# Beginning of a two-block kernel rebuilt: small modulation products, operands kept in PSUM, w_in chunks started earlier and in another order; attention part of the second block reordered

## The reference

```
# first block
mx = silu(c) @ ada_w + ada_b           # six modulation vectors of 1024: shift, scale, gate, ...
mc = silu(c_ctx) @ ada_w + ada_b       # only shift and scale are needed
hx = rmsnorm(x) * (1 + scale_x) + shift_x ;  hc = the same with ctx and mc
u = h @ w_in                           # q, forget gates (both directions), values, fourier part, gates
o = hgrn_bidir(...)                    # scan over x, started with the end states of a scan over ctx
y = (sigmoid(ga) * (fourier(u) @ w_a) + sigmoid(gb) * (readout(o) @ w_b)) @ w_out ; x = x + gate * y
x = x + gate2 * conv_ffn(modulate(rmsnorm(x), shift2, scale2)) ; x = rmsnorm(x)
# second block
p = rmsnorm(x) @ w_in_2                # q, k, v, three parts of a short convolution, u for pooling
mix = [band attention(q, k, v), short convolution, multiscale pooling(u)]
x = x + mix @ w_out_2 ; x = x + relu(rmsnorm(x) @ w_mlp1)**2 @ w_mlp2
```

## Time and profile before

| | us |
|---|---|
| median of 3 executions | 785.23 |
| fastest, slowest | 782.67, 795.02 |
| the profiled execution, its own time | 794.74 |
| its span in the trace | 792.9 |
| mean granted TensorE clock of the span | 0.976 |

### The profile page before, as it was taken

How to read it: one execution, slowest core, us unless ns; L and a number is a source line. 1 busy time by engine, 2 the same in 40 slices (tenths; PEclk the granted TensorE clock), 3 DMA queues, 4 the chain that set the end, 5 groups by cost and what they waited for, 6 DMA issues and landing times.

```text
span 792.9 us, 14202 instructions
## 1 busy us (share of the span) xinstructions
PE 748.9 (94%) x5892; PEld 715.1 (90%) x5892; DVE 548.5 (69%) x900; ACT 354.1 (45%) x417; POOL 434.0 (55%) x317
## 2 busy tenths in 40 slices
PE   8779999999989989999996998999699999999998
PEld 3468899999989989999996998999699999999998
DVE  5989994687563548987898878144965755565563
ACT  5445333454542555555534455434455433343331
POOL 0257642678679769899895987674738400000000
PEclk9889999999999989999998999999999999999999
DMA  9944345423676446446526554442315466545611
GB/s 376 420 163 173 143 179 213 161 84 131 215 263 211 150 169 246 160 167 259 216 104 266 229 198 165 152 160 107 112 59 203 150 224 212 169 176 187 213 54 54
DMA packets 20661, 144.63 MB, mean 182 GB/s; under 512 B 2291, under 2 KB 2547, under 8 KB 3445
## 3 DMA queue, kind: packets, MB, share of 16 engines
q1 hardware_dynamic: 20448, 143.64, 49.5%
q10 hardware_dynamic: 148, 0.07, 0.0%
HBM read 142.66 MB, written 1.05 MB: 181 GB/s over the span
## 4 chain that ended last, share of the span: by engine, by line
PE 67%; DVE 25%; ACT 3%; issue 3%; DMA 1%; POOL 1%; DVEq 0%; ACTq 0%
PE bank L1355 19%; PE bank L1357 18%; PE bank L1356 18%; DVE Y L1113 4%; DVE raw L877 4%; PE bank L1373 3%; PE bank L1463 2%; DVE XS L930 1%; DVE ada_s L823 1%; DVE F L921 1%; DVE wlo L393 1%; DVE K L931 1%; ACT whi L479 1%; PE bank L1387 1%; PE bank L1400 1%
## 5 line engine op out<-in xcount | busy, mean ns | idle before, releaser
L393 POOL TENSOR_TENSOR wlo<-raw,whi 128x512 fp32r<-128x512 f32 x306 | 428.7, 1438 | 196.0 <-ACT whi L479 193.3
L479 ACT ACTIVATE whi<-raw 128x2048 fp32r<-128x2048 f32 x107 | 204.0, 1908 | 46.9 <-PE bank L1357 34.8
L1113 DVE SCALAR_TENSOR_TENSOR Y<-bank,vec,Y 128x189 f32<-128x189 f32 (+2 forms) x352 | 122.8, 418 | 25.1 <-ACT Y L670 24.9
L1355 PE MATMUL bank<-H2h,whi 128*128 128x256 f32 x352 | 100.1, 284 | 9.2 <-POOL wlo L393 7.5
L1356 PE MATMUL bank<-H2l,whi 128*128 128x256 f32 x352 | 100.4, 285 | 0.0
L1357 PE MATMUL bank<-H2h,wlo 128*128 128x256 f32 x352 | 100.0, 284 | 0.0
L393 DVE TENSOR_TENSOR wlo<-raw,whi 128x2048 fp32r<-128x2048 f32 (+1 forms) x33 | 72.7, 2204 | 37.1 <-ACT whi L479 37.0
L1355 PE MATMUL bank<-H1h,whi 128*128 128x256 f32 (+1 forms) x288 | 91.3, 317 | 6.1 <-issue 4.6
L1356 PE MATMUL bank<-H1l,whi 128*128 128x256 f32 (+1 forms) x288 | 89.4, 311 | 0.0
L1357 PE MATMUL bank<-H1h,wlo 128*128 128x256 f32 (+1 forms) x288 | 89.3, 310 | 0.0
L1355 PEld LDWEIGHTS bank<-H2h,whi 128*128 128x128 f32 x352 | 68.1, 193 | 9.6 <-ACT whi L479 7.7
(11 more groups left out here) (265 smaller groups left out, 1853.1 us busy)
## 6 DMA issues: line engine op xcount, KB each, us to landing
raw<-in_w_mlp SPq DMA_DIRECT2D x32, 1024.0 KB, 4.9
raw<-in_w_in SPq DMA_DIRECT2D x30, 1024.0 KB, 4.9
raw<-in_ffn_up SPq DMA_DIRECT2D x22, 1024.0 KB, 4.9
raw<-in_ada_hi SPq DMA_DIRECT2D x16, 1024.0 KB, 4.9
raw<-in_ffn_down SPq DMA_DIRECT2D x11, 1024.0 KB, 5.0
raw<-in_w_out SPq DMA_DIRECT2D x8, 1024.0 KB, 4.8
ada_s<-in_ada_s SPq DMA_DIRECT2D x4, 1024.0 KB, 13.3
ada_p<-in_ada_p SPq DMA_DIRECT2D x3, 1024.0 KB, 13.2
```

The lines of the kernel that those rows point to most:

```text
L393: m = e.tensor_tensor(wlo[q % NHI][:, part], raw[place[split[q]] % NRAW][:, part], whi[q % NHI][:, part].bitcast(F32), ALU.subtract)
L479: e.activation(whi[q % NHI][:, :], raw[n % NRAW][:, :], ACT.Copy).then_inc(s["w_hi"], 1)
L1113: e.scalar_tensor_tensor(o[:, r0:r1, c0:c1], z[:, r0 + dr:r1 + dr, c0 + dc:c1 + dc], cw[:, f, tap:tap + 1], o[:, r0:r1, c0:c1], ALU.mult, ...
L1355: e.matmul(out, h[:, col:col + P], xh, start=first, stop=False, skip_group_check=True)
```

## The change

1. The shift products are turned round (`ada_columns`): the 128x128 piece of the chunk is the weight, the two columns of C2 are streamed, 16 products a chunk; the result lands in PSUM as it is needed. `MR` and `shift_turn` are gone. The sum of squares of x becomes 16 one-column products on PE; ACT squares x in four parts.
2. The rows of silu(c), the modulated tiles before rounding, the scan's states and the higher levels' gates are kept in PSUM banks; the dots of the beginning for x and 12 of the 16 `ada_hi` chunks read silu(c) from PSUM (`CP`). The forget gates' sigmoid is done in place in PSUM.
3. The loads of ada and w_in chunks are interleaved, and w_in is read in the order q (0, 1), fourier (2, 3), forget (4 to 7), values (8, 9), then as before. The `ada_hi` chunks stand behind w_in 5 to 10 (two each) and 16 to 19 (one each), and none in the FFN.
4. In the second block the pooling part of w_in_2 comes first and the values last; `pooling` is done early, and `turn_probabilities` stands between chunks.

The diff, cut to its core:

```diff
@@ -19,19 +19,18 @@
 NRAW, NHI = 4, 3
 PIECE = 512
 EPS = 1e-6
-SIDE = {**{i: 1 for i in range(3, 10)}, 16: 1, 17: 1, 18: 2, 19: 1}
-SIDE_FFN = (8, 11, 14, 17)
+SIDE = {**{i: 2 for i in range(5, 11)}, **{i: 1 for i in range(16, 20)}}
...
@@ -55,9 +53,6 @@
         plan += [(name, i, 2048) for i in range(n)]
     for i in range(22):
         plan.append(("ffn_up", i, 2048))
-        if i in SIDE_FFN:
-            plan.append(("ada_hi", side, 2048))
-            side += 1
         if i >= 5 and i % 2:
             plan.append(("ffn_down", (i - 5) // 2, 2048))
     plan += [("ffn_down", 9, 2048), ("ffn_down", 10, 2048)]
...
@@ -412,24 +417,28 @@
         def ada(name, i):
             e.dma_start(ada_buf[name, i][:, :], io[name][i]).then_inc(s[f"{name}{i}"], 16)
 
-        e.dma_start(vec[:, :], io["vec"]).then_inc(s["vec_in"], 16)
+        e.dma_start(vec[:, 0:NV1], io["vec"][:, 0:NV1]).then_inc(s["vec_in"], 16)
+        e.dma_start(XR[:, :, :], io["xT"]).then_inc(s["x_in"], 16)
+        ada("ada_p", 0)
         ada("ada_s", 0)
-        ada("ada_p", 0)
-        e.dma_start(XR[:, :, :], io["xT"]).then_inc(s["x_in"], 16)
+        ada("ada_p", 1)
         ada("ada_s", 1)
-        ada("ada_p", 1)
+        load(0)
+        ada("ada_p", 2)
+        ada("ada_p", 3)
         ada("ada_s", 2)
-        ada("ada_p", 2)
-        load(0)
         load(1)
         ada("ada_s", 3)
         load(2)
         e.dma_start(CX[:, :, :], io["ctxT"]).then_inc(s["ctx_in"], 16)
-        for n in range(3, 8):
-            load(n)
-        e.dma_start(MASKF[:, :, :], io["masks"]).then_inc(s["tables_in"], 16)
-        e.dma_start(con[:, P:NC], io["con"][:, P:NC]).then_inc(s["tables_in"], 16)
-        for n in range(8, len(plan)):
+        e.wait_ge(s["ada_dot"], 6)
+        load(3)
+        load(4)
...
@@ -488,46 +484,40 @@
         e.dma_start(CROW[:, 0:D], io["c_row"]).then_inc(s["c_in"], 16)
         e.dma_start(CROW[:, D:2 * D], io["c_ctx_row"]).then_inc(s["cctx_in"], 16)
         e.dma_start(ident, io["con"][:, 0:P]).then_inc(s["ident_in"], 16)
+        e.wait_ge(s["lb_step"], 2)
+        e.activation(LBE[:, :], LBE[:, :], ACT.Exp).then_inc(s["lb_exp"], 1)
         e.wait_ge(s["vec_in"], 16)
         e.activation(C2[:, :, :], v("c2").rearrange("p (k j) -> p k j", j=2), ACT.Silu).then_inc(s["c2_silu"], 1)
-        e.wait_ge(s["lb_step"], 2)
-        e.activation(LBE[:, :], LBE[:, :], ACT.Exp).then_inc(s["lb_exp"], 1)
-        for n in range(4):
-            row = CBX if n // 2 else CB
+        for n in range(2):
+            half = slice(n * 512, n * 512 + 512)
             e.wait_ge(s["c_spread"], n + 1)
-            e.activation(row[:, n % 2 * 512:n % 2 * 512 + 512], bank[misc_bank[f"c{n}"]][:, :],
-                         ACT.Silu).then_inc(s["c_silu"], 1)
+            e.activation(CB[:, half], CP[:, half], ACT.Silu).then_inc(s["c_row"], 1)
+            e.wait_ge(s["c_row"], n + 1)
+            e.activation(CP[:, half], CB[:, half], ACT.Copy).then_inc(s["c_silu"], 1)
+        for n in range(2):
+            e.wait_ge(s["c_spread"], n + 3)
+            e.activation(CBX[:, n * 512:n * 512 + 512], bank[n][:, :], ACT.Silu).then_inc(s["c_silu"], 1)
         e.wait_ge(s["x_in"], 16)
-        e.activation(HN[:, 0, :, :], XR[:, :, :], ACT.Square).then_inc(s["sq_in"], 1)
+        for i in range(4):
+            e.activation(SQI[:, 0, 2 * i:2 * i + 2, :], XR[:, 2 * i:2 * i + 2, :], ACT.Square).then_inc(s["sq_in"], 1)
...
@@ -815,13 +800,11 @@
             e.wait_ge(s["c_silu"], 2 * j + 2)
             r = ada_buf["ada_s", i]
             for f in range(2):
-                out = r[:, f * D:(f + 1) * D] if j else SPARE[f][:, :]
-                if j:
-                    e.wait_ge(s["ada_dot"], 4 * i + f + 1)
-                elif i:
-                    e.wait_ge(s["ada_dot"], 4 * i - 3 + f)
-                e.tensor_tensor_reduce(out=out, in0=r[:, f * D:(f + 1) * D], in1=(CBX if j else CB)[:, :], scale=1.0,
-                                       scalar=0.0, op0=ALU.mult, op1=ALU.add,
+                if dots[0] >= 2:
+                    e.wait_ge(s["ada_dot"], dots[0] - 1)
+                dots[0] += 1
+                e.tensor_tensor_reduce(out=SPARE[f][:, :], in0=r[:, f * D:(f + 1) * D], in1=(CBX if j else CP)[:, :],
+                                       scale=1.0, scalar=0.0, op0=ALU.mult, op1=ALU.add,
                                        accum_out=MOD[:, 8 + 2 * i + f, j:j + 1]).then_inc(s["ada_dot"], 1)
 
         steps = [0]
...
         ada_rows(0, 0)
+        reciprocal(2, 0, ("rms_in", 1), "rstd_in")
+        modulation(0)
+        input_tiles(0, XR, bank[5], [0, 1])
+        ada_rows(1, 0)
+        modulation(1)
+        input_tiles(0, XR, bank[5], [2, 3])
+        low(0)
         ada_rows(0, 1)
+        ada_rows(1, 1)
+        ada_rows(2, 0)
+        modulation(2)
+        input_tiles(0, XR, bank[5], [4, 5])
+        low(1)
+        ada_rows(3, 0)
+        modulation(3)
+        input_tiles(0, XR, bank[5], [6, 7])
+        low(2)
+        ada_rows(2, 1)
+        ada_rows(3, 1)
         for m, n in enumerate((4, 2, 1)):
             if m:
-                e.wait_ge(s["sum_x"], m)
+                e.wait_ge(s["sum_c"], m)
             else:
-                e.wait_ge(s["sq_in"], 1)
-            e.tensor_tensor(HN[:, 0, 0:n, :], HN[:, 0, 0:n, :], HN[:, 0, n:2 * n, :], ALU.add).then_inc(s["sum_x"], 1)
-        reciprocal(2, 0, ("rms_in", 1), "rstd_in")
-        ada_rows(1, 0)
-        ada_rows(1, 1)
-        modulation(0)
-        input_tiles(0, XR, bank[0], [0, 1])
-        modulation(1)
-        input_tiles(0, XR, bank[0], [2, 3])
-        ada_rows(2, 0)
-        ada_rows(2, 1)
-        low(0)
-        modulation(2)
-        input_tiles(0, XR, bank[0], [4, 5])
-        ada_rows(3, 0)
-        low(1)
-        modulation(3)
-        input_tiles(0, XR, bank[0], [6, 7])
-        ada_rows(3, 1)
-        low(2)
+                e.wait_ge(s["sq_in"], 5)
+            e.tensor_tensor(SQI[:, 1, 0:n, :], SQI[:, 1, 0:n, :], SQI[:, 1, n:2 * n, :], ALU.add).then_inc(s["sum_c"], 1)
...
         def decay(f):
             d, head = f // 4, f % 4
             pair = gates(d, head)
+            b = product("w_in", 4 + f // 2, f % 2)[:, :].rearrange("p (x t) -> p x t", x=2)
             e.wait_ge(s["f_sig"], f + 1)
-            e.tensor_scalar(pair, pair, LB1[:, head:head + 1], LB[:, head:head + 1], ALU.mult,
+            e.tensor_scalar(pair, b, LB1[:, head:head + 1], LB[:, head:head + 1], ALU.mult,
                             ALU.add).then_inc(s["f_gate"], 1)
...
@@ -1125,8 +1126,6 @@
                             ALU.subtract).then_inc(s["a_lo"], 1)
 
         for i in range(23):
-            if i in SIDE_FFN:
-                side(1)
             if i < 22:
                 convolve(i, 0)
...
@@ -1255,42 +1256,42 @@
 
         project_in(0)
         project_in(1)
-        qk_rstd(0)
-        project_in(2)
         e.wait_ge(s["h3_lo"], 8)
         e.wait_ge(s["sq2"], 4)
         for f in range(KT):
             e.scalar_tensor_tensor(XR[:, f, :], XR[:, f, :], v("final_g", f, 1), RR1[:, :], ALU.mult,
                                    ALU.mult).then_inc(s["x_norm"], 1)
+        project_in(2)
+        qk_rstd(0)
+        e.scalar_tensor_tensor(v("k_g"), v("q_g"), 0.125, v("k_g"), ALU.mult, ALU.mult).then_inc(s["x_norm"], 1)
+        pooling()
+        project_in(3)
         qk_rstd(1)
-        project_in(3)
-        e.scalar_tensor_tensor(v("k_g"), v("q_g"), 0.125, v("k_g"), ALU.mult, ALU.mult).then_inc(s["x_norm"], 1)
-        e.wait_ge(s["x_norm"], 9)
+        project_in(4)
         qk_rstd(2)
-        values_2(4)
-        k_norm(2)
-        qk_rstd(3)
-        values_2(5)
-        k_norm(3)
-        project_in(6)
-        scores(0)
-        project_in(7)
-        scores(1)
-        probabilities(0)
-        pooling()
-        probabilities(1)
-        project_in(8)
-        short_conv()
-        project_in(9)
         e.wait_ge(s["pool_mm"], 1)
         for f in range(2):
             e.tensor_scalar(UP[:, f, :], bank[misc_bank["pool"]][:, f * T:(f + 1) * T], v("pool_scale", f, 1), None,
                             ALU.mult).then_inc(s["pool_out"], 1)
         mix_low(UP[:, :, :], 6, 1)
+        qk_rstd(3)
+        project_in(5)
+        e.wait_ge(s["x_norm"], 9)
+        k_norm(2)
+        k_norm(3)
+        scores(0)
+        project_in(6)
+        scores(1)
+        probabilities(0)
+        project_in(7)
+        probabilities(1)
+        short_conv()
         e.wait_ge(s["conv_2"], 7)
         e.wait_ge(s["proj"], 8)
...
@@ -1384,36 +1387,35 @@
         for n in range(4):
             if n % 2 == 0:
                 e.wait_ge(s[("c_in", "cctx_in")[n // 2]], 16)
-            e.matmul(misc(f"c{n}")[:, :], ones[0:1, 0:P], CROW[:, n * 512:n * 512 + 512], start=True,
+            e.matmul(bank[(3, 4, 0, 1)[n]][:, :], ones[0:1, 0:P], CROW[:, n * 512:n * 512 + 512], start=True,
                      stop=True).then_inc(s["c_spread"], 1)
 
```

(116 more changed lines are left out.)

393 lines of the change are left out of this document (200 added, 193 removed).

## The result

| | kernel before | kernel after |
|---|---|---|
| median, first 20 executions of each | 790.42 | 782.18 |
| lowest | 782.67 | 779.48 |
| the profiled execution, its own time | 794.74 | 779.48 |
| its span | 792.9 | 777.2 |
| mean granted clock | 0.976 | 0.989 |

The account below looks back on a forecast made before the run. PE, busy 94% of 792.9 us, was taken as the bound through its stalls and lowered clock; 3.1 - 1.5 - 4.1 - 9.6 - 6.5 = -18.6 from the profiled 794.7 gave 776.1, forecast 776, range 763 to 786.

Parts of the forecast that it names:

- A: The beginning, to the first chunk for x and ctx together: 72.3 us against 69.2, +3.1; bounds -8 and +5.
- B: From the first joint chunk to w_a: small stalls of 1.9 us go, 0.4 comes, -1.5 (0 to -4).
- D: FFN without dots: a stall behind one held-up dot goes, -9.6 us against the profile, 0 against the median.
- a median that holds the stall: Sign of a wrong prediction: the median before does hold the FFN stall, then 766 us.
- the clock under small products: In the beginning, small products run at half clock until tiles of w_in run: 6.8 us for 32 records.
- the tail on DVE: End of the beginning: four ctx dots 4.6 us, 2 more with POOL, sums 2.4, low part 1.2, until 66.6.
- The bound (+5): Upper bound for the beginning, +5 us, if POOL blocks DVE at each low part.
- C: w_a: 2.6 us of waiting for ACT and 1.5 of half clock go, -4.1 (0 to -4.5).
- E: Second block: wait for scores -6.65 us, half clock -2, a tail that stays +2: -6.5; bounds -3 and -9.
- 1, quick small products: Beginning: with the clock up a set costs 3.5 us instead of 6.8, time 765 to 766; chance 0.22.
- 2, the lock-out that moves: Behind w_in 16 to 19, one dot held up by POOL delays the scan's readout: 786 or 790 us; chance 0.08.
- 3, the rebuilt start costs as much as the rest gives: Beginning at +8 us, second block -3, w_a 0, PE idling until ada chunks come: 785; chance 0.14.

Follow-up runs that it names:

- The exchange on DVE: The kernel before with pooling() moved after the second half of the softmax on DVE, nothing else changed: ratio 1.003 (0.997 to 1.008).

## Why the prediction was right and wrong

In the profile's terms 776.1 was forecast and 779.5 measured: A came out 5.8 us worse, w_b and w_out 1.1, B 3.0 better and D 0.8; the median lies another 2.7 us above this quickest execution.

**D, right, with its reading of the median wrong.** The dot that POOL holds off is what it was said to be, -10.4 for -9.6. That the median lacks it was an inference from three executions. In five series of the kernel before, 10 of 20, 11 of 35, and 5, 7 and 4 of 11 executions took over 791 us; a third to two thirds have it, 37 of 88 in all, and the median of a series lies between 787.7 and 793.3 by how many do. The two groups are 6 to 9 us apart, so D is worth some 3 us on the mean. The prediction named a median that holds the stall as a sign that it is wrong.

**A, the failed step: +3.1 forecast, +8.9 and +10.8 measured.** The half of it that looked risky, the clock under small products, came out as forecast: sets of 6.97 us for 6.8, the fourth tile done at 43.6 for 44.3, low part 2 even earlier (done at 54.8, where the sum has 56.4). What was mis-sized is the tail on DVE, "four dots against ctx (4.6, with POOL 2 more), the sums for ctx (2.4 ...), low part 3 of 1.2": 7.9 for 6.6, 5.4 for 2.4, 2.3 for 1.2, which with the early start makes 3.7 us. All three read two operands in SBUF beside POOL, and the sums were priced by the earlier trace rows, where POOL was still idle. Before, POOL itself did these sums. Then, behind the wait for them, the clock was down, and the fourth chunk took 7.8 us for 5.7: the other 2.1. The bound (+5) had the cause and not the size.

**B, right in sign, three times too small.** The stalls in it (1.9 and 0.3 us) went, and no wait of PE is left between 78.1 and 238.9; of the other 2.3 us some 2 are not a stall but the pitch of the products, the time from one start to the next (last section), which the sum did not have.

**C and E, right** to 0.2 us each. E's price for the tail that stays (2 us) was 2.9 of wait, without the half clock. The exchange on DVE shows that DVE's order alone does not do it; that the new chunk order did follows from what is left.

**w_b and w_out**, +1.1, were not in the sum.

**Rivals.** 1, quick small products: no, a set took 6.97 us. Its price was too large as well: with half of the products left out a set took 3.55, which is its condition, and the first 512-column product came 6.3 us earlier and the time fell by 7, where it had 10.8 for both; its 765 was not reached. 2, the lock-out that moves: not in the kernel after, whose longest dot with CB behind w_in 16 to 19 took 2.3 us and delayed nothing on PE; put back in the FFN it returned. 3, the rebuilt start costs as much as the rest gives: it had A right (+8 for +8.9), for another reason than its late loads, but C and E came in full. Its 785 doesn't follow from its own terms, 785.2 + 8 - 1.5 - 3 = 788.7, above the stated range. Against the rule of the Trainium skill (page "SBUF — State Buffer", section "Who interferes with whom") that the pair is held for one instruction, the dot of 13.16 to 13.17 us is now seen in three profiles of three kernels. The same section of the Trainium skill has it that a DVE instruction with at most one SBUF input does not contend; the dots with CP agree, 1217 ns on the mean and none over 1.22 us beside a busy POOL.

## What to carry to other kernels

A DVE instruction with two SBUF operands beside a POOL that works without gaps can last as long as POOL's whole run of pieces: take one operand from PSUM, or keep it out of such stretches, and take a price for it only from rows where POOL is busy too. Judge a kernel's median by enough executions to see whether it has groups. Small products on PE in the beginning cost twice here: at half clock themselves (6.97 us a set), and in the half clock of the tiles behind them. The form with 256 columns took 3.61 us once the clock was up, but it pays only where PE and not DVE is the chain. Before crediting an edit with the last 2 or 3 us, compare two profiles stretch by stretch: the clock and the pitch far from the edit can give or take as much.
